# A 32-byte tensor ahead of the overlaid SBUF tensors of a hybrid retention, SSD and mixture-of-experts kernel

## The reference, cut to what matters

```
for layer in range(2):
    h = rmsnorm(x, norm1_w[layer])
    x = x + hybrid_mixer(h, ...)          # retention + SSD + stick-breaking attention
    h = rmsnorm(x, norm2_w[layer])
    f = swiglu(h, wg, wu, wd) if layer == 0 else moe_swiglu(h, router_w, wg, wu, wd)
    x = x + f
return rmsnorm(x, final_norm_w)

def swiglu(h, wg, wu, wd):
    return (silu(h @ wg) * (h @ wu)) @ wd

def moe_swiglu(h, router_w, wg, wu, wd):
    # softmax over the two largest router logits gives combine[token, expert]
    return sum(combine[..., e:e+1] * swiglu(h, wg[e], wu[e], wd[e]) for e in range(8))
```

## Time and profile before

| | |
|---|---|
| median of 3 runs | 1539.08 us (1535.33 to 1540.57) |
| the profiled execution: first to last instruction | 1532.9 us |
| its own time as a run | not given apart from the three above; 6.2 us lie between the span and the median |
| TensorE matmuls busy | 1500.0 us, 98% |
| VectorE busy | 1176.8 us, 77% |
| ScalarE busy | 982.9 us, 64% |
| from HBM | 435.59 MB, 285 GB/s over the span |
| mixer 0 and dense part | 0 to about 360 us |
| mixer 1 and routing | about 360 to 534 us |
| mixture of experts | 534 to about 1525 us |

### The profile page before, as it was taken

One profiled execution on the slowest core, in us unless ns is written; L12 is line 12 of the kernel. 1 busy time (PEld: TensorE's weight loads), 2 busy tenths in 40 slices (PEclk: granted clock), 3 DMA queues, 4 the chain that ended last, 5 costly groups with the idle time before them and its releaser, 6 DMA issues.

```text
span 1532.9 us, 19288 instructions
## 1 busy us (share of the span) xinstructions
PE 1500.0 (98%) x7343; PEld 1241.4 (81%) x7347; DVE 1176.8 (77%) x846; ACT 982.9 (64%) x759; POOL 45.7 (3%) x50
## 2 busy tenths in 40 slices
PE   7999999999999999999999999999999999999997
PEld 5987788888888678888888888887888888888886
DVE  4777454444787588898878889878889888888886
ACT  4565433344556477777777777776777777677774
POOL 2000000000000000000100000200000200000010
PEclk9999999999999999999999999999999999999999
DMA  9624555554552379999999999999999999999992
GB/s 314 218 96 145 174 193 189 190 192 138 169 176 98 108 261 381 371 360 372 362 341 331 376 373 345 374 344 330 367 373 359 362 375 341 344 369 376 349 376 109
DMA packets 190584, 437.70 MB, mean 286 GB/s; under 512 B 9329, under 2 KB 13473, under 8 KB 190385
## 3 DMA queue, kind: packets, MB, share of 16 engines
q1 hardware_dynamic: 189024, 432.90, 78.7%
q0 software_dynamic: 1056, 2.19, 0.7%
q10 hardware_dynamic: 432, 1.57, 0.3%
HBM read 435.59 MB, written 1.05 MB: 285 GB/s over the span
## 4 chain that ended last, share of the span: by engine, by line
PE 94%; DVE 3%; ACT 1%; DMA 1%; issue 1%; SPq 0%; DVEq 0%; ACTq 0%
PE ps L1250 29%; PE ps L1252 28%; PE ps L1251 28%; PE ps L1554 2%; PE ps L1511 1%; DVE w_lo L787 1%; DMA raw<-in_w_in_dram 1%; PE ps L1529 0%; PE ps L1530 0%; PE ps L1313 0%; PE ps L1312 0%; PE ps L1311 0%; ACT w_hi L456 0%; PE ps L1704 0%; PE ps L1305 0%
## 5 line engine op out<-in xcount | busy, mean ns | idle before, releaser
L1095 DVE TENSOR_TENSOR w_lo<-raw,w_hi 128x2048 fp32r<-128x2048 f32 x333 | 754.8, 2290 | 122.3 <-ACT w_hi L604 121.4
L604 ACT ACTIVATE w_hi<-raw 128x2048 fp32r<-128x2048 f32 x332 | 630.5, 1920 | 171.5 <-PE ps L1252 171.5
L1250 PE MATMUL ps<-w_hi,aT_hi 128*128 128x512 f32 (+1 forms) x1296 | 512.8, 396 | 14.0 <-DVE w_lo L787 5.8
L1252 PE MATMUL ps<-w_hi,aT_lo 128*128 128x512 f32 (+1 forms) x1296 | 504.3, 389 | 0.0
L1251 PE MATMUL ps<-w_lo,aT_hi 128*128 128x512 f32 (+1 forms) x1296 | 503.0, 388 | 0.0
L1250 PEld LDWEIGHTS ps<-w_hi,aT_hi 128*128 128x128 f32 x1296 | 243.9, 188 | 68.2 <-issue 11.3
L1252 PEld LDWEIGHTS ps<-w_hi,aT_lo 128*128 128x128 f32 x1296 | 243.9, 188 | 53.0
L1251 PEld LDWEIGHTS ps<-w_lo,aT_hi 128*128 128x128 f32 x1296 | 244.2, 188 | 48.5
L787 DVE TENSOR_TENSOR w_lo<-raw,w_hi 128x2048 fp32r<-128x2048 f32 (+2 forms) x81 | 177.0, 2186 | 114.3 <-ACT w_hi L456 114.2
L456 ACT ACTIVATE w_hi<-raw 128x2048 fp32r<-128x2048 f32 (+2 forms) x81 | 148.2, 1831 | 117.3 <-PE ps L1252 111.0
L1250 PE MATMUL ps<-w_hi,s2T_hi 128*128 128x512 f32 x544 | 213.8, 393 | 0.0
(11 more groups left out here) (269 smaller groups left out, 924.1 us busy)
## 6 DMA issues: line engine op xcount, KB each, us to landing
raw<-in_moe_w_gate_dram SPq DMA_DIRECT2D x112, 1024.0 KB, 6.9
raw<-in_moe_w_up_dram SPq DMA_DIRECT2D x112, 1024.0 KB, 7.5
raw<-in_moe_w_down_dram SPq DMA_DIRECT2D x112, 1024.0 KB, 6.9
raw<-in_w_in_dram SPq DMA_DIRECT2D x20, 1024.0 KB, 5.6
raw<-in_ffn_w_gate_dram SPq DMA_DIRECT2D x14, 1024.0 KB, 5.1
raw<-in_ffn_w_up_dram SPq DMA_DIRECT2D x14, 1024.0 KB, 5.0
raw<-in_ffn_w_down_dram SPq DMA_DIRECT2D x14, 1024.0 KB, 4.8
raw<-in_w_out_dram SPq DMA_DIRECT2D x8, 1024.0 KB, 5.0
```

The costliest lines, as they stand in the source:

```text
L604: nc.scalar.activation(moe_hi(pos), raw[:, slot, :], ACT.Copy).then_inc(hi_ready, 1)
L1095: V.tensor_tensor(moe_lo(pos), raw[:, pos % 6, :], moe_hi(pos).bitcast(F32), ALU.subtract)\
L1250: mm(out, lhs_hi, rhs_hi, start=start, stop=False, skip_group_check=True)
L1252: return mm(out, lhs_lo, rhs_hi, start=False, stop=stop, skip_group_check=True)
```

## The change

One line is added, behind `zeros` and ahead of the overlays. Nothing reads or writes the new tensor.

More of the change, by code:

```diff
@@ L141, in hybrid_kernel @@
         zeros = sb("zeros", [P, P], BF16)
+        align64 = sb("align64", [P, 8])
         mixing = ExitStack()
```

## The result

| | before | with the change |
|---|---|---|
| median of 21 runs | 1537.03 us (1533.63 to 1540.57) | 1534.22 us (1530.40 to 1538.36) |
| ratio | | 0.998, 95% interval 0.9971 to 0.9989 |
| first to last instruction | 1532.9 us | 1533.2 us |
| TensorE matmuls busy | 1500.0 us | 1500.2 us |
| two items (10 and 11), transposes to transposes | 33.90 us | 33.83 us |

The account below looks back on a forecast made before the run. The prediction took TensorE's matmuls to bound the kernel. It summed 9.2 us for the fourth pair and its trail and 0.3 us for the scatter to 9.5 us, from 1539.1 to 1529.6 us, range 1525 to 1537.

Parts of the forecast that it names:

- What bounds the kernel: Whole kernel: TensorE's matmuls, busy 98% of the span; in the mixture of experts each nanosecond saved on them shortens the end.
- The price of a sub in the fourth pair, by buffer: Mixture of experts: a plain sub costs 2.72 us, one in the fourth pair 0.08 more, the sub behind it 0.04 more.
- the second way to the sum: Two items against a dense step with aligned buffers: 33.90 us would become 33.56; 0.34 us, 28 times, is 9.5 us.
- Why I put it down to the start address: Fourth pair, 32 bytes past a multiple of 64: each 2048-byte row takes one 64-byte unit more, 6.9 ns a matmul.
- fourth pair to a multiple of 64: Matmuls of the 84 subs in the fourth pair each lose their 6.9 ns excess: 6.9 us gained.
- This trail goes when its cause goes: Slow first matmuls of the sub behind one in the fourth pair vanish with the fourth pair's cost: 2.2 us gained.
- The scatter: Its 72 matmuls, with y_hi and y_lo moving from 32 past 64, gain 4 ns each: 0.3 us.
- For the unit speaks nothing: Fourth pair: a unit of 128 bytes was dismissed as cause, since the excess was 16 columns, not 32.
- Rival 1: Fourth pair: its place in memory or a 128-byte unit makes the 6.9 ns; no gain, 1539.1 us. Chance 12%.
- Can the others keep up: Mixture of experts: VectorE needs 30.3 us of a 33.56 us step, and DMAs at 375 GB/s are not at a limit.
- Rivals 2 and 3: Loads give TensorE's gain back, 1537.2 us, chance 3%; moved mixer tensors slow VectorE and ScalarE, 1543.8 us, chance 3%.
- the first 534 us as before within 1 us: Sign in the profile after: the part ahead of the mixture of experts keeps its length within 1 us.

Follow-up runs that it names:

- pad224_again: The pad224 kernel (224 unused bytes) timed once more, beside the change itself on one chip: 1529.88 us, ratio 0.9937 to the kernel before.
- stat32: Against the changed kernel, stationary tensors and fourth pair moved to 160 past a multiple of 256, the other moving buffers left in place: 1551.77 us in one run.
- pad224: The changed kernel with an unused tensor of 224 bytes, fourth pair 128 past a multiple of 256: 1528.67 us, ratio 0.9955 to the kernel before.
- shift32: Against the changed kernel, two unused tensors put weight buffers and stationary tensors 160 past a multiple of 256, every difference 0: 1530.96 us, ratio 0.9957 to before.
- pad96: The changed kernel with an unused tensor of 96 bytes, fourth pair at a multiple of 256: 1536.25 us, ratio 1.0002 to the kernel before.
- bench2: TensorE alone, no model, moving and stationary starts varied: differences of 256, 288, 320 and 384 bytes gave 226.7, 233.3, 228.8 and 233.3 ns a matmul.

## Why the prediction was wrong

- **What bounds the kernel: right.** TensorE is the one waited for in the profiles, and 28 times what two items gain or lose comes within about 1 us of what the stage does, the two profiles with a lower clock inside the stage aside (pad224_again 8.4 us by items, 8.1 by the stage; stat32 10.1 and 9.0).
- **The price of a sub in the fourth pair, by buffer: right.** 6.9 ns a matmul and a trail behind it. pad224 shows that both were there to be had, and nearly as large as the second way to the sum said: two items at 33.60 us against 33.56 forecast, a stage 8.1 us shorter against 9.5. In its other profile it was 5.9, for a reason that stands below.
- **"Why I put it down to the start address": the step that failed.** 6.9 ns are 16.5 columns, and I read them as one 64-byte unit more a row, so that any multiple of 64 would do. The runs show that it isn't the moving operand's own start: shift32, with all buffers 32 past a multiple of 64, runs at 226.7 ns a matmul, pad96, at a multiple of 256, at 233. It is its distance to the stationary operand's start. The change took that distance from 32 to 64, where TensorE alone loses 2.2 ns in place of 6.7. So the term "fourth pair to a multiple of 64", put at 6.9 us, came out at 84 times 0.04 = 3.4 us.
- **"This trail goes when its cause goes": right in pad224, useless here**, since the cause stayed at a smaller size. The forecast of 2.2 us for it came out at nothing or a little less: sub 64 takes 2.77 us after 2.76, which is 56 times 0.01 = 0.6 us lost.
- **The scatter: a misreading.** I took its 0.23 and 0.24 us for a cost of its own. `y_hi` and `selT` lie in the same overlay, 32 past 64 both, so that their distance is 0. By theory D these rows show a trail, behind a restart or a sub of the fourth pair. The traces bear that out: the distance between the two operands is 0 in every kernel, and the mean distance from a scatter matmul to the next one is 233.7 ns before, 233.4 with the change and 230.8 in pad224, where the trails of the fourth pair are gone. The 0.3 us of this term came out at 0.
- **"For the unit speaks nothing": too sure.** The trace before held one address off the others' phase, and that address had three properties (past 64, past 128, past the stationary's phase) that one point can't tell apart. Rival 1 ("the offset is not the cause, or not this one") named this at 12% and gave no middle outcome; what came is between it and the forecast. The rule of the Trainium skill that I had set beside it, 16-byte cachelines in "SBUF — State Buffer", section "Specifications (TRN2)", would have made the change worth nothing; the measured gain, small as it is, differs from that too, and neither rule speaks of two operands.
- **Can the others keep up: right.** 326 loads still wait for VectorE, in the fastest version the steps are 33.60 us and no split waits for a load.
- **Rivals 2 and 3: right to be small.** The splits and `cv` kept their durations, and no load became late.
- **The time inside the range: partly luck.** The sum started from 1539.1 us, the median of three runs; 21 runs give 1537.0. From there the same 9.5 us lead to 1527.5, and the miss is 6.7 us and not 4.6. The range held because it had been stretched toward no change. Its near end rests on a slip, too: 6.9 less 0.8 is 6.1 and not 6.3 us, which changes nothing. And "the first 534 us as before within 1 us" failed by 2.9 us in a profile with a lower granted clock there, which says nothing of the change.

**What stays open.** Why the two starts interfere is not shown. That the load of the next stationary operand is read beside the moving stream and gets in its way is what I would try first, and it is only argued. One sign for it stands in bench2's stream with one stationary operand of three off by 32:

```profile
285.69 0.40 PE L89 MATMUL ps<-zero,stat_zero 128*128 128x512 f32 x1
285.69 0.19 PEld L90 LDWEIGHTS ps<-zero,stat_thirtytwo 128*128 128x128 f32 x1
285.93 0.39 PE L90 MATMUL ps<-zero,stat_thirtytwo 128*128 128x512 f32 x1
...
286.16 0.40 PE L88 MATMUL ps<-zero,stat_zero 128*128 128x512 f32 x1
...
286.39 0.40 PE L89 MATMUL ps<-zero,stat_zero 128*128 128x512 f32 x1
```

The longest distance of the three, 0.24 us (239 ns), is the one in which the stationary operand off by 32 is loaded for the next matmul. The matmul that then uses it stands only 229 ns ahead of its successor. The third, 232 ns, is above 226.7 too, so this is no proof. Steps of 16 bytes (112) gave two results. Why TensorE needs some matmuls to find its pace again is open as well.

## What to carry to other kernels

In an fp32r matmul stream with 512 moving columns, give moving and stationary tensors starts that are equal within 256 bytes; a small odd-sized tensor between them is enough to lose it, and a few unused bytes restore it (here 0.45 to 0.63% for 224 bytes a partition). In bf16, or with 256 columns or fewer, a difference of 0 was nowhere faster than 32, 64 or 128: leave it. And when one buffer of several is slow in the trace, list every property in which its address differs, its distance to the other operand of the instruction included, and test a range of starts before you trust a rule that fits one.

## What the runs showed of the hardware

- TensorE alone, fp32r, 512 columns: 226.7 ns a matmul at a difference of 0 or 256 between moving and stationary start, 228.8 at 64 and 320, 233.3 at most others, 234.2 at 160. One stationary operand of three off by 32 puts all three above 226.7 (229, 232 and 239).
- At the first two turns from one pair of experts to the next TensorE sits idle for 1.2 to 1.9 us. In two of nine profiles, pad224's and shift32's, some eight matmuls behind the first turn ran at the lower of the two clocks, 1.2 GHz. The stretches of pad224 and of the same kernel in pad224_again, columns as in the earlier trace rows:

```profile
794.00:806.00 12.00, 10.12 (x40) 7.86 (x39) 8.12 (x5) 5.37 (x6) 0.00 (x0) 0.86 0.94 341
```

```profile
794.00:806.00 12.00, 10.38 (x48) 8.28 (x47) 9.92 (x8) 7.26 (x7) 0.00 (x0) 1.00 0.96 346
```

A granted clock of 0.86 in the one and of 1.00 in the other, 40 matmuls against 48. The rows of the slow ones:

```profile
796.71 0.49 PE L1251 MATMUL ps<-w_hi,aT_hi 128*128 128x512 f32 x1 [1.88 <-issue]
...
797.82 0.63 PE L1252 MATMUL ps<-w_lo,aT_hi 128*128 128x512 f32 x1
798.25 0.63 PE L1253 MATMUL ps<-w_hi,aT_lo 128*128 128x512 f32 x1
```

From 797.82 to 798.25 it is 0.43 us instead of 0.23. There are seven such distances and a shorter one at either end, 1.6 us lost in all. That is most of the 2.1 us by which the stage of the first pad224 profile is longer than that of the second. The idle time before was 1.88 us there and 1.62 in the second, but its length doesn't settle it: shift32 fell after 1.80 us, and pad96 kept its full clock after 1.84. So the drop belongs to no kernel of these.
